# One hybrid decoder step in fp32 on one core: x tiles in buffers of their own and latents projected by thirds of tokens, the sample rows' output projection in column groups, a closing norm in fused passes

## The reference

```
p = x @ w_in                                   # b_g, c_g, h, cq, ckv, kr, g_conv, g_attn
ckv = rmsnorm(p[ckv]);  q = rmsnorm(p[cq]) @ w_uq;  kr = rope(p[kr])
o  = attention(q, ckv, kr)                     # causal for the prompt, paged cache for the samples
m  = sigmoid(g_conv) * (b_g * conv3(c_g * h)) @ w_br_conv + sigmoid(g_attn) * o @ w_br_attn
h1 = layernorm(ALPHA * x + m @ w_o) * ln1_g + ln1_b
e1, e2 = top 2 of 8 experts in the best of 4 groups, by h1 @ router weights
y  = layernorm(ALPHA * h1 + sum_k w_k * expert_k(h1)) * ln2_g + ln2_b
```

## Time and profile before

| | |
|---|---|
| median of 3 runs | 1933.38 us (1933.15 to 1934.62) |
| the profiled execution, its own time | 1921.72 us |
| its span in the profile | 1920.0 us |
| mean granted TensorE clock | 0.955 of full |
| TensorE matmul busy | 1771.1 us, 92% of the span |
| VectorE busy | 541.4 us, 28% |
| ScalarE busy | 338.0 us, 18% |
| GpSimd busy | 185.6 us, 10% |

### The profile page before, as it was taken

How to read it: one execution, slowest core, us unless ns; L and a number is a source line. 1 busy time by engine, 2 the same in 40 slices (tenths; PEclk the granted TensorE clock), 3 DMA queues, 4 the chain that set the end, 5 groups by cost and what they waited for, 6 DMA issues and landing times.

```text
span 1920.0 us, 19292 instructions
## 1 busy us (share of the span) xinstructions
PE 1771.1 (92%) x7943; PEld 1008.2 (53%) x7944; DVE 541.4 (28%) x1059; ACT 338.0 (18%) x623; POOL 185.6 (10%) x177
## 2 busy tenths in 40 slices
PE   7999999999999999999999999389999999999970
PEld 5556666666666665665765444344444444444430
DVE  1333242424232222323122554701111111111117
ACT  1013323232321212121120010101111110111112
POOL 1000000000013121110000000001111111111114
PEclk8999999999999999999899999579999999999995
DMA  6101121121136344230533521458999999999934
GB/s 194 44 19 40 45 56 45 33 63 37 45 102 196 121 160 170 110 110 1 187 132 110 201 77 56 157 215 339 364 389 378 370 393 367 396 359 395 364 80 176
DMA packets 103960, 340.48 MB, mean 177 GB/s; under 512 B 23834, under 2 KB 67938, under 8 KB 87492
## 3 DMA queue, kind: packets, MB, share of 16 engines
q1 hardware_dynamic: 88372, 274.11, 37.5%
q0 software_dynamic: 14336, 60.95, 10.4%
q10 hardware_dynamic: 1168, 4.23, 0.5%
HBM read 308.42 MB, written 36.03 MB: 179 GB/s over the span
## 4 chain that ended last, share of the span: by engine, by line
PE 90%; DVE 4%; DMA 3%; ACT 1%; issue 1%; another core or an unknown queue 1%; POOL 0%; POOLq 0%; SPq 0%; ACTq 0%; DVEq 0%
PE psum L1185 15%; PE psum L871 12%; PE psum L979 8%; PE psum L1202 7%; PE psum L1140 7%; PE psum L1131 6%; PE psum L799 5%; PE psum L1190 4%; PE psum L908 3%; PE psum L1016 3%; PE psum L881 2%; PE psum L1208 2%; PE psum L926 2%; PE psum L1180 2%; PE psum L915 2%; PE psum L1063 1%
## 5 line engine op out<-in xcount | busy, mean ns | idle before, releaser
L1185 PE MATMUL psum<-arena 128*128 128x512 f32 x640 | 283.5, 602 | 1.0 <-DVE arena L1927 1.0
L871 PE MATMUL psum<-arena 128*128 128x344 f32 x768 | 244.9, 456 | 0.0
L979 PE MATMUL psum<-arena 128*128 128x344 f32 x576 | 188.4, 466 | 13.6 <-DVE arena L1679 5.7
L1185 PEld LDWEIGHTS psum<-arena 128*128 128x128 f32 x640 | 121.7, 193 | 148.4 <-issue 147.6
L871 PEld LDWEIGHTS psum<-arena 128*128 128x128 f32 x768 | 137.9, 190 | 63.8 <-issue 8.6
L979 PEld LDWEIGHTS psum<-arena 128*128 128x128 f32 x576 | 104.4, 193 | 71.7 <-issue 33.1
L1202 PE MATMUL psum<-arena 128*128 128x512 f32 x320 | 141.4, 595 | 0.0
L1140 PE MATMUL psum<-arena 128*128 128x512 f32 (+1 forms) x288 | 132.3, 620 | 2.8 <-DVE arena L1774 2.8
L1131 PE MATMUL psum<-arena 128*128 128x344 f32 x384 | 113.2, 458 | 1.1 <-ACT arena L1437 1.1
L1131 PEld LDWEIGHTS psum<-arena 128*128 128x128 f32 x384 | 74.0, 193 | 40.3 <-issue 3.0
L704 POOL DMA_INDIRECT arena<-in_cache_ckv,arena x32 | 30.5, 954 | 668.1 <-DVE arena L1614 485.0
(11 more groups left out here) (309 smaller groups left out, 1787.4 us busy)
## 6 DMA issues: line engine op xcount, KB each, us to landing
arena<-in_w_gate SPq DMA_DIRECT2D x32, 2048.0 KB, 12.5
arena<-in_w_up SPq DMA_DIRECT2D x32, 2048.0 KB, 17.0
arena<-in_w_down SPq DMA_DIRECT2D x32, 2048.0 KB, 20.9
arena<-in_w_in SPq DMA_DIRECT2D x33, 512.0 KB, 4.3
gates<-arena SPq DMA_DIRECT2D x16, 516.0 KB, 5.1
arena<-gates SPq DMA_DIRECT2D x16, 516.0 KB, 5.4
arena<-in_x_prompt SPq DMA_DIRECT2D x16, 512.0 KB, 4.5
arena<-in_w_o SPq DMA_DIRECT2D x1, 4096.0 KB, 17.1
```

The costliest lines, as they stand in the source:

```text
L871: ins = mm(out, wring[:, s, k, :], xT[:, k, b * SP3:(b + 1) * SP3], start=(k == 0), stop=(k == KD - 1))
L979: ins = mm(psum[:, FB + t, 0:SP3], wring[:, u, k, :], xT[:, k, t * SP3:(t + 1) * SP3], start=(k == 0), stop=(k == KD - 1))
L1185: ins = mm(psum[:, bank, :], xgT[:, xpar, k, :], w[:, k, :], start=(k == 0), stop=(k == KD - 1))
```

## The change

Three stretches are written anew; nothing between them is touched.

1. The opening. Each x tile has a buffer of its own (`x_in[t]`), and SP waits for the landing of tile t-3 in place of the transposes of it. The block 0 weights go behind x tile 2, the block 1 weights behind x tile 5. TensorE transposes three tiles, waits for both copies, and runs the 16 matmuls of that third of the tokens for blocks 0 and 1; then the next three. The transposes have one pair of banks (6 and 7) in place of two, since blocks 0 and 1 hold banks 0 to 5. The loads of the heads' weights (`load_heads(0)`) wait for the last transpose, since their buffers lie where x is.
2. `out_proj` of the sample tile: 32 matmuls of 8 by 256 columns, four column groups of the array that write partitions 0, 32, 64 and 96 of one bank, in place of 16 of 8 by 512. VectorE gathers the four pieces with four copies (L1831) before the residual is added.
3. The closing norm. ScalarE takes the mean (Copy with an accumulator) and the mean square (Square with an accumulator) of a tile. VectorE makes the negative variance, (v - mean) * ln2_g in one pass, the reciprocal, and v / deviation + ln2_b in one pass. GpSimd has no part in it. The sample tile comes first, then tiles 0 to 7.

```diff
@@ opening, SyncE
             def load_x(t):
                 r = rows_of(t)
                 if t >= 3:
-                    sp.wait_ge(xt_done, 2 * (t - 2))
+                    sp.wait_ge(x_ld[t % 3], 16 * (t // 3))
-                sp.dma_start(x_in[0:r, t % 3, :], src).then_inc(x_ld[t % 3], 16)
-
-            for t in range(2):
-                load_x(t)
+                sp.dma_start(x_in[t][0:r], src).then_inc(x_ld[t % 3], 16)
...
+            for t in range(3):
+                load_x(t)
             load_w(0, C_KV)
+            for t in range(3, 6):
+                load_x(t)
             load_w(1, C_KV + P)
-            for t in range(2, NT):
+            for t in range(6, NT):
                 load_x(t)
...
+            sp.wait_ge(xt_done, 2 * NT)
             load_heads(0)
@@ opening, TensorE
+            def turn_x(t):
+
                 r = rows_of(t)
                 pe.wait_ge(x_ld[t % 3], 16 * (t // 3 + 1))
                 for g in range(2):
-                    if t >= 2:
-                        pe.wait_ge((xt_act, xt_dve)[g], t - 1)
+                    if t:
+                        pe.wait_ge((xt_act, xt_dve)[g], t)
                     for k in range(4):
...
+                        ins = nc.tensor.transpose(psum[:, 6 + g, k * P:k * P + r], x_in[t][0:r, (4 * g + k) * P:(4 * g + k + 1) * P], ident[0:r, 0:r])
                     ins.then_inc(xt_done, 1)
-            pe.wait_ge(xt_act, NT)
-            pe.wait_ge(xt_dve, NT)
+
+            for b in range(3):
+                for t in range(3 * b, 3 * b + 3):
+                    turn_x(t)
+                pe.wait_ge(xt_act, 3 * b + 3)
+                pe.wait_ge(xt_dve, 3 * b + 3)
+                for n in range(2):
+                    pe.wait_ge(w_ld[n], 16)
+                    for k in range(KD):
+                        ins = mm(psum[:, 3 * n + b, 0:SP3], wring[:, n, k, :], xT[:, k, b * SP3:(b + 1) * SP3], start=(k == 0), stop=(k == KD - 1))
+                    if b == 2:
+                        ins.then_inc(proj_done, 1)
@@ output projection, TensorE
+                if t == NT - 1:
+                    for k in range(KD):
+                        for q in range(4):
+                            ins = mm(psum[32 * q:32 * q + NS, 2 * (t % 2), 0:CL], mT[:, k, SEQ:T], wo_sb[:, k, q * CL:(q + 1) * CL],
+                                     start=(k == 0), stop=(k == KD - 1), skip_group_check=True)
+                    ins.then_inc(wo_done, 1)
+                    return
@@ norm1, VectorE
+                mixed = psum[0:r, 2 * s:2 * s + 2, :].rearrange("p b n -> p (b n)")
+                if t == NT - 1:
+                    mixed = v
+                    for q in range(4):
+                        link(nc.vector.tensor_copy(v[:, q * CL:(q + 1) * CL], psum[32 * q:32 * q + NS, 2 * s, 0:CL]))
+                stt(out=v, in0=xr[0:r, t % 3, :], scalar=ALPHA, in1=mixed, op0=ALU.mult, op1=ALU.add).then_inc(r_dve, 1)
@@ closing norm: GpSimd
-            for t in range(NT):
-                v = fin[0:rows_of(t), t, :]
-                pool.wait_ge(g_dve, t + 1)
-                pool.tensor_tensor(v, v, ln2b[0:rows_of(t)], ALU.add).then_inc(f_pool, 1)
@@ closing norm: ScalarE (LAST = [8, 0, 1, ..., 7])
-                nc.scalar.activation(rsm[0:r, t % 2, 1:2], rsm[0:r, t % 2, 0:1], ACT.Sqrt).then_inc(sd_act, 1)
-                act.wait_ge(nb_dve, t + 1)
-                nc.scalar.activation(v, v, ACT.Identity, bias=rsm[0:r, t % 2, 3:4], scale=rsm[0:r, t % 2, 2:3]).then_inc(n_act, 1)
+            def moments(n):
+
+                t = LAST[n]
+                r = rows_of(t)
+                act.wait_ge(f_ld[t], F_BASE[t] + 16)
+                if n:
+                    act.wait_ge(mom_act, 2 * n)
+                nc.scalar.activation(waste[0][0:r], fin[0:r, t, :], ACT.Copy, scale=1.0 / D, accum_out=mean9[0:r, t:t + 1]).then_inc(mom_act, 1)
+                nc.scalar.activation(waste[1][0:r], fin[0:r, t, :], ACT.Square, scale=D ** -0.5, accum_out=sq9[0:r, t:t + 1]).then_inc(mom_act, 1)
+
+            def deviation(n):
+
+                t = LAST[n]
+                r = rows_of(t)
+                act.wait_ge(var_dve, NT + n + 1)
+                nc.scalar.activation(sd9[0:r, t, 1:2], sd9[0:r, t, 0:1], ACT.Sqrt, bias=eps[0:r], scale=-1.0).then_inc(sd_act, 1)
+
+            act.wait_ge(rows_out, 16 * NE)
+            moments(0)
+            for n in range(NT):
+                if n + 1 < NT:
+                    moments(n + 1)
+                deviation(n)
@@ closing norm: VectorE (in place of summed, factors and scaled)
+                dve.wait_ge(mom_act, 2 * n + 2)
+                stt(out=sd9[0:r, t, 0:1], in0=mean, scalar=mean, in1=sq9[0:r, t:t + 1], op0=ALU.mult, op1=ALU.subtract).then_inc(var_dve, 1)
+                stt(out=v, in0=v, scalar=mean, in1=ln2g[0:r], op0=ALU.subtract, op1=ALU.mult).then_inc(g_dve, 1)
...
+                dve.wait_ge(sd_act, NT + n + 1)
+                link(nc.vector.reciprocal(sd9[0:r, t, 0:1], sd9[0:r, t, 1:2]))
+                dve.wait_ge(g_dve, n + 1)
+                stt(out=v, in0=v, scalar=sd9[0:r, t, 0:1], in1=ln2b[0:r], op0=ALU.mult, op1=ALU.add).then_inc(f_dve, 1)
+
+            for n in range(NT):
+                centred(n)
+                if n:
+                    finished(n - 1)
+            finished(NT - 1)
```

More of the change, by code:

```diff
@@ L124, in build @@
         z = Zone(Z2, Z3)
-        kr_tmp = z(2, T)
-        x_in = z(3, D)
+        x_in = [z(D) for _ in range(NT - 1)] + [at(Z3, D)]
+        kr_tmp = at(Z3 + D, 2, T)
         z = Zone(Z3, Z4)
@@ L382, in build @@
         ah_act, ah_out = sem("ah_act"), [sem("ah_out0"), sem("ah_out1")]
+        LAST = [NT - 1] + list(range(NT - 1))
+        waste = [xgT[:, 0, :, :].rearrange("p k n -> p (k n)"), xgT[:, 1, :, :].rearrange("p k n -> p (k n)")]
         gates = nc.dram_tensor("gates", (KD, 2, P, T), F32).ap()
@@ L641, in _ @@
             sp.wait_ge(h_out, 16 * NT)
-            for t in range(NT):
+            for t in LAST:
                 r = rows_of(t)
                 sp.dma_start(fin[0:r, t, :], sums[t * P:t * P + r, :]).then_inc(f_ld[t], 16)
-            for t in range(NT):
-                sp.wait_ge(f_pool, t + 1)
+            for n, t in enumerate(LAST):
+                sp.wait_ge(f_dve, n + 1)
                 dst = a["y_prompt"][0, t * P:(t + 1) * P, :] if t < NT - 1 else a["y_sample"][:, 0, :]
@@ L771, in _ @@
             pool.memset(pad_row, 0.0).then_inc(sums_whole, 1)
-            pool.wait_ge(ln1_ld, 96 + 32)
-            for t in range(NT):
-                v = fin[0:rows_of(t), t, :]
-                pool.wait_ge(g_dve, t + 1)
-                pool.tensor_tensor(v, v, ln2b[0:rows_of(t)], ALU.add).then_inc(f_pool, 1)
         @block.tensor
@@ L809, in square_sums @@
                 ins.then_inc(proj_done, 1)
-            for n in range(NPRE):
-                if n >= 2:
-                    pe.wait_ge(setev[n % 2], n // 2)
+            for n in range(2, NPRE):
+                pe.wait_ge(setev[n % 2], n // 2)
                 if n in (SUM_KV, SUM_Q):
@@ L1795, in norm1 @@
                 dve.wait_ge(wo_done, t + 1)
-                stt(out=v, in0=xr[0:r, t % 3, :], scalar=ALPHA, in1=psum[0:r, 2 * s:2 * s + 2, :].rearrange("p b n -> p (b n)"), op0=ALU.mult, op1=ALU.add).then_inc(r_dve, 1)
+                mixed = psum[0:r, 2 * s:2 * s + 2, :].rearrange("p b n -> p (b n)")
[4 more added lines that the diff above has]
+                stt(out=v, in0=xr[0:r, t % 3, :], scalar=ALPHA, in1=mixed, op0=ALU.mult, op1=ALU.add).then_inc(r_dve, 1)
                 dve.wait_ge(r_dve, t + 1)
@@ L1964, in _, with centred, finished @@
             dve.wait_ge(ln1_ld, 96 + 32)
[L1966 to L1979 removed]
+            link(nc.vector.memset(eps, LN_EPS))
+            def centred(n):
+                t = LAST[n]
                 r = rows_of(t)
                 v = fin[0:r, t, :]
[L1982 to L1992 removed]
+                mean = mean9[0:r, t:t + 1]
+                dve.wait_ge(mom_act, 2 * n + 2)
+                stt(out=sd9[0:r, t, 0:1], in0=mean, scalar=mean, in1=sq9[0:r, t:t + 1], op0=ALU.mult, op1=ALU.subtract).then_inc(var_dve, 1)
+                stt(out=v, in0=v, scalar=mean, in1=ln2g[0:r], op0=ALU.subtract, op1=ALU.mult).then_inc(g_dve, 1)
+            def finished(n):
+                t = LAST[n]
+                r = rows_of(t)
+                v = fin[0:r, t, :]
+                dve.wait_ge(sd_act, NT + n + 1)
[7 more added lines that the diff above has]
+            finished(NT - 1)
 INS = ["x_prompt", "x_sample", "cache_ckv", "cache_krope", "state_conv", "page_table", "w_in", "conv_w", "q_norm_g",
```

34 lines of the change are left out of this document (4 added, 30 removed).

## The result

| kernel | median of its runs | interval of the ratio to the kernel before |
|---|---|---|
| before | 1932.76 us (1930.63 to 1934.62, 6 runs) | |
| changed | 1901.39 us (1897.43 to 1902.14, 6 runs) | 0.9842, 95% [0.9831, 0.9852] |

The change saves 31.4 us where 21.4 were forecast. Of the three parts, two came out near their sums and the third, the closing norm, at more than twice its sum.

What follows compares the result with a forecast made beforehand. TensorE, busy 92%, loses time waiting for x, in the 8-row output projection (VectorE idle) and in the closing norm, where it has no work. Savings 7.7 + 7.2 + 6.5 = 21.4 us: 1933.4 - 21.4 = 1912.0, range 1903 to 1922.

Steps and rivals of the forecast that it cites:

- From there 6.73 to the end of the span as before: Closing norm: the end keeps its 6.73 us, plus 1.3 for a 512 KB last store, giving 1913.5.
- Rival (b): Closing norm: ScalarE becomes the bound at some 3.6 us a tile, paying 2.3 not 6.5: 1916; chance 0.06.
- its 6.5: Closing norm: forecast saving of 6.5 us, with both ScalarE and VectorE at 2.95 a tile.
- that rule: Closing norm: GpSimd shares SBUF interfaces with VectorE and contends with instructions of two SBUF inputs.
- My sentence that both fused passes would have been exposed: Closing norm: had GpSimd kept its addition, both fused VectorE passes, taken at 1.28 us each, would have met its contention.
- Rival (a): Opening: stays bound by transfers, block 1's weights late, TensorE idle then at half clock; pays 2.5: 1917; chance 0.08.
- Rival (c): Opening: the split keeps TensorE at the lower clock, 20.8 us later, kernel 1940; chance 0.03.
- My bound for half clock: Output projection of the sample rows: all 32 matmuls at half clock take 7.3 us, saving 6.5.
- Subtracting from the median: Whole kernel: saving summed on the profiled execution (1921.72 us) but taken unscaled from the median of 1933.38.
- rival (d): Whole kernel: the change does nothing, a later wait, such as for cache pages, taking the gain back; chance 0.03.
- the three bounds: Savings: opening 2.5 to 10.3, output projection 6.5 to 7.4, closing norm 3.0 to 8.5; added, 12.0 to 26.2.
- best case of 8.5: Closing norm: cheapest case, passes of 1.070 and a hidden store, saving 8.5 us.

Runs made afterwards that it cites:

- before again: The kernel before with no edit, profiled a second time on another chip: 1911.78 us, ratio 1.0004.
- opening alone: The kernel before with only the opening's part (load order, nine buffers, transposes in banks 6 and 7, projections by thirds): ratio 0.9954.
- output projection alone: The kernel before with only the sample rows' output projection in column groups: ratio 0.9967.
- small operation: The changed kernel with a 128 by 1 GpSimd fill at its end, waiting for VectorE's last pass: 1884.41 us, ratio 0.9861.
- bias on GpSimd: The changed kernel with the closing bias added by GpSimd again, VectorE's second pass only multiplying: 1914.97 us, ratio 0.9912.
- GpSimd one tile ahead of VectorE: The kernel before with the last tile's bias (8 rows) added by VectorE, the other eight tiles' by GpSimd: ratio 0.9996.
- GpSimd's wait: The changed kernel where GpSimd waits at its end for VectorE's last pass and does nothing more: 1904.13 us in one run.
- closing norm alone: The kernel before with only the closing norm's part of the change: ratio 0.9934.
- changed again: The changed kernel with no edit, on the second chip: 1879.10 us, ratio 0.9836.
- two edits more: The changed kernel with next third's transposes between groups of four projection matmuls and an early one-column square root: 1873.33 us, ratio 0.9802.
- late weights: The changed kernel with block 1's weights issued behind the last x tile, not behind tile 5: 1906.03 us, ratio 0.9879.
- store of 32 KB: The changed kernel with closing tiles in natural order, so the first load is 512 KB: 1899.38 us, ratio 0.9833.

## Why the prediction was wrong

**The step that failed** is in the closing norm: "From there 6.73 to the end of the span as before, and 1.3 more since the last store is 512 KB". I carried the 6.73 over as if it belonged to the last store, though the operation that ends there was GpSimd's, and the change takes GpSimd out. It measured 3.25 in place of 8.03: 4.8 us, nearly half of the 10 that are missing. All fourteen traces show what it was:

| last of the kernel | its end to the end of the span |
|---|---|
| GpSimd: before, before again, opening alone, output projection alone, small operation, bias on GpSimd | 6.73, 6.72, 6.69, 6.74, 6.71, 6.71 |
| GpSimd one tile ahead of VectorE | 6.7 from GpSimd, 4.4 from VectorE |
| GpSimd's wait | 6.9 |
| VectorE, store of 512 KB: changed, closing norm alone, changed again, two edits more, late weights | 3.25, 3.25, 3.26, 3.25, 3.25 |
| VectorE, store of 32 KB | 2.4 |

The row that should have made me ask was in the views that I read: SP's wait of 4.5 us in the last barrier. I took it for part of the constant.

**The passes of the closing norm**: from the first operation to the end of the last 28.7 us, where I had 31.55, 2.8 less. The mechanism was right, the size off. The accumulating passes are of 1.05, not 1.12, and the readout of 0.19 lies within them for half; a tile costs ScalarE 2.28 and VectorE 2.72 where I had 2.95 for both. I took the pass's price from a row that reads PSUM although one that reads SBUF at 1.070 stood beside it. Rival (b), ScalarE as the bound, is therefore far off. The first load was 0.3 cheaper than taken. 4.8, 2.8 and 0.3 make the 7.9 us by which this part saved more than its 6.5.

My reading of what paced this stretch before was incomplete. A tile took 3.57 us there: GpSimd's addition of 2.34 and VectorE's product of 1.21, one after the other. The run with the bias on GpSimd shows that they exclude each other. I had used that rule only to defend VectorE's new price, but it also explains the old one. My sentence that both fused passes would have been exposed was not tried as it stands, since only the first is fused in that run. That one came ahead of GpSimd and made it wait; the product behind it stood although it had one input.

**The opening**: 9.0 us for 7.7 between the first two profiles, within its bounds. Over all traces the two are nearer: with the old opening the copy of block 1 begins at 56.0 to 58.6 (five traces, mean 57.4), with the new one at 48.4 to 50.6 (seven, mean 49.1), which is 8.3 us. The order of things was as forecast. Block 1's weights landed at 16.02 in place of 17.3 (1.3), and no time went to half clock (0.5); against that a matmul took 0.593 for 0.58, 0.5 over 40 of them. Rival (a) did not occur: the wait was 0.57. That it lies close is shown by the late weights, where it cost 6.5. Rival (c), the lower clock for all of the opening, fell: even an idle time of 4.77 cost only 1.7 behind it.

**The output projection**: 7.3 us for 7.2. In four of the nine traces with column groups the run took 5.33 us and not 3.64, and the distance from tile 7's residual to the positions was 26.3 to 26.4 us in all nine. My bound for half clock, 7.3 us, had covered that.

**The sum against the median**: 9.0 + 7.3 + 14.4 = 30.7. Subtracting from the median was right, and rival (d) fell: on one chip the parts alone have 0.9954, 0.9967 and 0.9934. The stretch where the two profiles differ by 13.4 us differs by 10.2 with the kernel unchanged (347.7 and 337.5), though perhaps only from chip to chip. That the change does not lengthen it where the waits for "remote" occur rests on the medians: 0.9842 with these waits, 0.9836 without.

**The range** added the three bounds, but the closing norm's best case of 8.5 held the 6.73 fixed. With an open end term it would have reached 4.8 us lower.

## What to carry to other kernels

Ask of every term that is "as before" which engine it belongs to, and whether the change removes that engine's part: the last microseconds belonged here to GpSimd's end. By these numbers, as an estimate, GpSimd costs nothing at the end of this kernel if it is done some 3.5 us before VectorE's last pass ends (6.7 less 3.25), or 4.3 where the last store is of 32 KB (6.7 less 2.4). Where GpSimd and VectorE work on SBUF at once, add their times if a trace shows one ending just behind the other; don't take the larger. And before two profiles are subtracted, compare them stretch by stretch: 13 us of difference stood in a part that nothing had touched.

## What the hardware showed that was not expected

- The span ends 6.7 to 6.9 us after GpSimd's last instruction (eight traces), whether it was an addition, a fill of 0.10 us or only a wait; behind VectorE's last, with GpSimd long done, 3.25.
- A VectorE product with one input of 128 by 1024 took 0.75 us alone and 2.65 beside GpSimd's addition; VectorE's statistics of 512 columns took 0.68 to 0.70 in the kernel before, GpSimd at work or not.
- The sample attention lasts 337 us on two chips and 347.7 to 361 on the others, with the same instructions. The difference goes with waits for "remote". In the changed kernel's first profile VectorE's copy stood 7.26 us until 678.81, 1.1 us after the last of eight indirect loads that GpSimd issues in a row (676.74, 0.95 us long); TensorE's transposes for it had ended near 674.3:

```profile
676.74 0.95 POOL L709 DMA_INDIRECT arena<-in_cache_krope,arena  x1 [0.30 <-issue]
...
678.81 0.69 DVE L1721 COPY arena<-psum 128x512 f32<-128x512 f32 x1 [7.26 <-remote]
```

  That the burst holds the copy up is suggested by this order alone; no run tried it, and why some chips don't show it stays open.
- TensorE's clock can fall for a moment without a long idle time ahead of it: in the second profile of the changed kernel the last third's run of 16 matmuls (32 records) took 11.18 us in place of 9.49, with this window in it (granted clock 0.50, the lower of the two levels). Between the transposes ahead of it TensorE had stood 0.33 us at most at a time, and the first profile, with the same rows there, has no such fall:

```profile
40.00:42.00 2.00, 2.00 (x5) 1.13 (x4) 0.00 (x0) 0.00 (x0) 0.00 (x0) 0.50 0.55 102
```
